# Expert layers of a two-block model: token gather and router with the narrow operand stationary in four column groups

## The reference

```python
def expert_choice_moe(h, w_router, w_gate, w_up, w_down):
    b, s, _ = h.shape
    cap = EC_FACTOR * s // N_EXPERTS
    logits = jnp.einsum('bsd,de->bse', h, w_router, preferred_element_type=jnp.float32)
    aff = jax.nn.softmax(logits, axis=-1)
    gates, idx = lax.top_k(aff.transpose(0, 2, 1), cap)
    b_ix = jnp.arange(b)[:, None, None]
    xs = h[b_ix, idx]
    a = jnp.einsum('becd,edf->becf', xs, w_gate)
    u = jnp.einsum('becd,edf->becf', xs, w_up)
    y = jnp.einsum('becf,efd->becd', jax.nn.silu(a) * u, w_down)
    y = y * gates[..., None].astype(y.dtype)
    return jnp.zeros_like(h).at[b_ix, idx].add(y)
```

## Time and profile before

| | us |
|---|---|
| median of three runs | 2250.71 |
| lowest, highest | 2247.79, 2253.75 |
| span of the profiled execution, first to last instruction | 2245.6 |
| busy in it: PE matmuls, PE weight loads, DVE, ACT | 2025.5, 1382.8, 894.7, 718.1 |
| mean granted TensorE clock (1.00 is 2.4 GHz, 0.50 is 1.2 GHz) | 0.936 |
| moved by DMA, mean rate | 592.33 MB, 264 GB/s |

### The profile page before, as it was taken

The page is one execution under the profiler, slowest core; times in us unless marked ns, Lnnn a source line. Parts: engine busy times, 40 slices in busy tenths (PEclk is TensorE's granted clock), DMA queues, the critical chain, the costliest instruction groups (busy, mean ns, idle before and its releaser), DMA issues.

```text
span 2245.6 us, 38410 instructions
## 1 busy us (share of the span) xinstructions
PE 2025.5 (90%) x17052; PEld 1382.8 (62%) x17052; DVE 894.7 (40%) x1280; ACT 718.1 (32%) x1015; POOL 40.7 (2%) x65
## 2 busy tenths in 40 slices
PE   7999988887879999987777879999999999999998
PEld 6888433333327887433333329575899796758996
DVE  6444211010106444111111117547677475476774
ACT  5444111111115454111111115424444453244442
POOL 1000000000001000000000000000000000000000
PEclk9999898788889999888888889999999999999999
DMA  9246899999997256999999996023754360227540
GB/s 325 74 152 261 370 426 429 429 428 427 429 427 274 75 188 281 385 428 428 428 429 428 428 413 246 16 79 112 236 188 169 103 232 4 89 101 228 187 178 19
DMA packets 139668, 592.33 MB, mean 264 GB/s; under 512 B 5745, under 2 KB 59201, under 8 KB 114449
## 3 DMA queue, kind: packets, MB, share of 16 engines
q1 hardware_dynamic: 138432, 586.67, 65.9%
q0 software_dynamic: 1104, 3.70, 0.5%
HBM read 589.30 MB, written 1.05 MB: 263 GB/s over the span
## 4 chain that ended last, share of the span: by engine, by line
PE 68%; DMA 24%; DVE 3%; ACT 2%; issue 1%; SPq 1%; DVEq 0%; POOLq 0%; ACTq 0%; POOL 0%
PE ps L578 36%; DMA ring<-in_w_up 23%; PE ps L1182 11%; PE ps L2191 3%; PE ps L2006 2%; PE ps L904 2%; PE ps L2240 1%; PE ps L1205 1%; PE ps L1144 1%; DMA ring<-in_w_in 1%; PE ps L1214 1%; PE ps L595 1%; PE ps L1003 1%; PE ps L1099 1%; PE ps L1079 1%
## 5 line engine op out<-in xcount | busy, mean ns | idle before, releaser
L1182 PE MATMUL ps<-ring,area 128*32 128x512 f32 x1920 | 308.0, 714 | 124.5 <-DMA ring<-in_w_up 124.5
L554 DVE TENSOR_TENSOR ring_lo<-ring,slab_hi 128x2048 fp32r<-128x2048 f32 x136 | 311.3, 2291 | 227.0 <-ACT slab_hi L549 226.9
L549 ACT ACTIVATE slab_hi<-ring 128x2048 fp32r<-128x2048 f32 x136 | 260.0, 1913 | 287.2 <-PE ps L578 266.3
L1182 PEld LDWEIGHTS ps<-ring,area 128*32 128x32 f32 x1920 | 72.8, 128 | 314.5 <-DMA ring<-in_w_up 156.7
L578 PE MATMUL ps<-hT_hi,slab_hi 128*128 128x256 f32 x832 | 234.7, 282 | 3.0 <-DVE hT_lo L571 1.5
L578 PE MATMUL ps<-hT_lo,slab_hi 128*128 128x256 f32 x832 | 233.4, 280 | 0.0
L578 PE MATMUL ps<-hT_hi,ring_lo 128*128 128x256 f32 x832 | 232.5, 280 | 0.0
L1771 DVE TENSOR_TENSOR area<-ps,par 128x256 f32<-128x256 f32 x32 | 13.6, 424 | 480.2 <-PE ps L1144 480.2
L1421 ACT ACTIVATE area<-ps 128x512 f32<-128x512 f32 x32 | 19.1, 597 | 536.9 <-PE ps L1182 536.9
L1205 PE MATMUL ps<-ring,area 128*32 128x512 f32 x992 | 158.1, 794 | 31.6 <-DVE area L1791 29.8
L578 PEld LDWEIGHTS ps<-hT_hi,slab_hi 128*128 128x128 f32 x832 | 156.0, 188 | 4.2 <-issue 2.2
(11 more groups left out here) (384 smaller groups left out, 3147.6 us busy)
## 6 DMA issues: line engine op xcount, KB each, us to landing
ring<-in_w_up SPq DMA_DIRECT2D x62, 2048.0 KB, 20.4
ring<-in_w_down SPq DMA_DIRECT2D x62, 2048.0 KB, 21.6
ring<-in_w_gate SPq DMA_DIRECT2D x56, 2048.0 KB, 15.2
ring<-in_w_ffn_up SPq DMA_DIRECT2D x44, 1024.0 KB, 7.8
ring<-in_w_in SPq DMA_DIRECT2D x18, 2048.0 KB, 10.1
ring<-in_w_ffn_down SPq DMA_DIRECT2D x10, 2048.0 KB, 7.8
ring<-in_xattn_w_kv SPq DMA_DIRECT2D x8, 2048.0 KB, 16.7
area<-in_w_gate SPq DMA_DIRECT2D x6, 2048.0 KB, 15.1
```

Source lines behind the costliest of these rows:

```text
L549: return m.nc.scalar.activation(hi, whole, ACT.Copy)
L554: return m.nc.vector.tensor_tensor(lo, whole, hi, ALU.subtract)
L1182: ins = mm(ps[32 * g:32 * g + CAP, 1, :], m.tokT[:, k, :], gate_up[i][:, k % 4, (g % 2) * BANK:(g % 2 + 1) * BANK], start=k == 0, stop=k = ...
```

## The change

Four edits, all in the experts:

1. The router turns its operands round: 32 router columns (those of two neighbouring chunks, of which one half is what is wanted) are stationary, 256 tokens of `hT` move, in four column groups of the array, one chunk each; the second half adds to the same PSUM bank. DVE copies the 128x256 result to SBUF, and two matmuls with a constant `expert_sum` add the four groups and turn them. One of the four copies of the residual (`into_sums`) stands before these two, another behind them; the other two stay behind the turn of the affinities.
2. The gather turns its operands round too: `onehot` (32 columns) stationary, 256 features of `xn` moving, four column groups, 8 matmuls. DVE copies the result to SBUF (`tok_rows`), PE turns it with two transposes (`turn_tokens`), and DVE scales it into `tokT`. In the loop these transposes stand behind those of gate and up.
3. The first maxima and the first replacement of the search read PSUM directly; the copy goes.
4. For expert 0 the turn of `gated` is issued behind the eighth matmul of gate and up instead of ahead of the first.

```diff
+    def into_sums(nh, t):
+        mm(ps[:, 4 + 2 * nh + t, :], m.ident, m.x[:, t, nh * BANK:(nh + 1) * BANK], start=True, stop=False, skip_group_check=True)
...
-        for t in range(NT):
-            for k in range(4 * half, 4 * half + 4):
-                ins = mm(ps[:, 4 + t, 0:E], m.hT[:, k, t * P:(t + 1) * P], router[:, k, :], start=k == 0, stop=k == KD - 1)
+        for g in range(4):
+            k = 4 * half + g
+            ins = mm(ps[CAP * g:CAP * g + CAP, 4, 0:T], router[:, (k - g % 2) * E:(k - g % 2) * E + CAP], m.hT[:, k, :],
+                     start=half == 0, stop=half == 1)
...
+    into_sums(1, 0)
+    pe.wait_ge(*at("router_rows", l))
+    for t in range(NT):
+        ins = mm(ps[:, 5, t * E:(t + 1) * E], m.router_rows[:, t * P:(t + 1) * P], m.const("expert_sum"), start=True, stop=True)
+    ins.then_inc(s("router_full"), 1)
+    into_sums(1, 1)
     pe.wait_ge(*at("aff_rows", l))
...
-        for k in range(KD):
-            for t in range(NT):
-                ins = mm(ps[:, 2, k * CAP:(k + 1) * CAP], m.xn[:, t, k * P:(k + 1) * P], m.onehot[:, t, :],
+        for t in range(NT):
+            for g in range(4):
+                ins = mm(ps[CAP * g:CAP * g + CAP, 2, 0:T], m.onehot[:, t, :], m.xn[:, t, g * T:(g + 1) * T],
                          start=t == 0, stop=t == NT - 1)
...
+    def turn_tokens(n):
+        pe.wait_ge(s("tok_rows"), n)
+        for c in range(2):
+            ins = nc.tensor.transpose(ps[:, 2, T + c * P:T + (c + 1) * P], m.tok_rows[:, c * P:(c + 1) * P], m.ident)
+        ins.then_inc(s("tokens_T"), 1)
...
-        pe.wait_ge(s("gated"), n)
-        for t in range(NT):
-            ins = nc.tensor.transpose(ps[:, 3, t * P:(t + 1) * P], m.gated[:, t, :], m.ident)
-        ins.then_inc(s("pick_T"), 1)
+        if not first:
+            turn_places(n)
...
                 if first and k == 1 and g == 3:
                     ins.then_inc(s("first_rows_used"), 1)
+                    turn_places(n)
...
         ins.then_inc(m.s("gu_T"), 1)
+        if not last:
+            turn_tokens(n + 1)
         pe.wait_ge(m.s("hid_cols"), n)
...
-    v.tensor_copy(work[:, 0, :], ps[0:E, 0, 0:T])
-    dve.drain()
     for r in range(CAP // 8):
-        v.max(best, work[:, r % 2, :])
+        left = work[:, r % 2, :] if r else ps[0:E, 0, 0:T]
+        v.max(best, left)
         dve.drain()
-        v.match_replace(work[:, 1 - r % 2, :], best, work[:, r % 2, :], -1.0)
+        v.match_replace(work[:, 1 - r % 2, :], best, left, -1.0)
...
         dve.wait_ge(s("tok_full"), n)
-        v.tensor_tensor(m.tokT, ps[:, 2, 0:KD * CAP].rearrange("p (k c) -> p k c", c=CAP), bc(m.par1("ffn_g"), CAP), ALU.mult)\
-            .then_inc(s("tok_cols"), 1)
+        v.tensor_copy(m.tok_rows, ps[:, 2, 0:T]).then_inc(s("tok_rows"), 1)
+        dve.wait_ge(s("tokens_T"), n)
+        v.tensor_tensor(m.tokT.rearrange("p (g c) n -> p c g n", c=2), ps[:, 2, T:].rearrange("p (c g n) -> p c g n", c=2, n=CAP),
+                        bc(m.par1("ffn_g").rearrange("p (g c) -> p c g", c=2), CAP), ALU.mult).then_inc(s("tok_cols"), 1)
```

More of the change, by code:

```diff
@@ L144, in constants @@
     put("iota_slot", np.broadcast_to(i % CAP + 1, (P, P)))
+    even = np.arange(E) == i[:, None] % CAP
+    odd = np.arange(E) == i[:, None] % CAP - E
+    put("expert_sum", np.where((i[:, None] // CAP) % 2 == 0, even, odd))
     put("causal", np.where(i[None, :] <= i[:, None], 0.0, -1e30))
@@ L316 @@
 group("mem_dve", first=[("xs_max", 2), ("xp_rows", 2), ("xpT_d", 2), ("xo_cols_d", 4)])
-group("route_pe", first=[("router_full", 2), ("aff_T", 1), ("top_T", 1)])
+group("route_pe", first=[("router_parts", 1), ("router_full", 1), ("aff_T", 1), ("top_T", 1)])
 group("route_act", first=[("router_exp", 2)])
 group("x_perm", first=[("x_perm", 4)])
-group("route_dve", first=[("router_max", 1), ("aff_rows", 1), ("top_found", 1), ("topc_set", 1)])
+group("route_dve", first=[("router_rows", 1), ("router_max", 1), ("aff_rows", 1), ("top_found", 1), ("topc_set", 1)])
 group("acc_full", first=[("acc_full", 2)])
-for n in ("onehot", "gated", "tok_full", "pick_T", "gu_full", "gu_T", "tok_cols", "hid_cols", "pick", "gu_rows", "gate_silu",
+for n in ("onehot", "gated", "tok_full", "tok_rows", "tokens_T", "pick_T", "gu_full", "gu_T", "tok_cols", "hid_cols", "pick", "gu_rows", "gate_silu",
           "dn_rows_a", "dn_rows_d"):
@@ L1111, in tensor_experts @@
     mm = nc.tensor.matmul
-    router = m.par1("router").rearrange("p (k e) -> p k e", e=E)
+    router = m.par1("router")
+    def into_sums(nh, t):
+        mm(ps[:, 4 + 2 * nh + t, :], m.ident, m.x[:, t, nh * BANK:(nh + 1) * BANK], start=True, stop=False, skip_group_check=True)
     for half in range(2):
@@ L1128, in tensor_experts @@
     ins.then_inc(s("aff_T"), 1)
-    for nh in range(2):
-        for t in range(NT):
-            mm(ps[:, 4 + 2 * nh + t, :], m.ident, m.x[:, t, nh * BANK:(nh + 1) * BANK], start=True, stop=False,
-               skip_group_check=True)
+    for t in range(NT):
+        into_sums(0, t)
     pe.wait_ge(*at("top_found", l))
@@ L1141, in gather, with turn_places @@
         pe.wait_ge(s("onehot"), n)
-        for k in range(KD):
-            for t in range(NT):
-                ins = mm(ps[:, 2, k * CAP:(k + 1) * CAP], m.xn[:, t, k * P:(k + 1) * P], m.onehot[:, t, :],
+        for t in range(NT):
+            for g in range(4):
+                ins = mm(ps[CAP * g:CAP * g + CAP, 2, 0:T], m.onehot[:, t, :], m.xn[:, t, g * T:(g + 1) * T],
                          start=t == 0, stop=t == NT - 1)
-                if behind_up and k == 0 and t == 0:
+                if behind_up and g == 0 and t == 0:
                     ins.then_inc(m.free[3], 1)
         ins.then_inc(s("tok_full"), 1)
+    def turn_tokens(n):
[3 more added lines that the diff above has]
+        ins.then_inc(s("tokens_T"), 1)
+    def turn_places(n):
+        pe.wait_ge(s("gated"), n)
+        for t in range(NT):
+            ins = nc.tensor.transpose(ps[:, 3, t * P:(t + 1) * P], m.gated[:, t, :], m.ident)
+        ins.then_inc(s("pick_T"), 1)
     def expert(e, first=False, second=False, third=False, last=False):
@@ L1222, in tensor_experts @@
     gather(l * E + 1, behind_up=False)
+    turn_tokens(l * E + 1)
     expert(0, first=True)
```

18 lines of the change are left out of this document (10 added, 8 removed).

## The result

The changed kernel takes 2238.66 us in the median of four runs (2235.53 to 2242.52), the kernel before, beside it, 2252.23 (2247.79 to 2255.91): a ratio of 0.9949, 95% interval 0.9930 to 0.9967. Three more sets of runs gave 0.9938 (0.9924 to 0.9952), 0.9951 (0.9934 to 0.9968) and 0.9951 (0.9935 to 0.9966). The two profiled executions tell less: spans of 2245.6 and 2237.9 us, 7.7 apart. The profiled execution of the changed kernel took 2239.7 us, so 1.8 us lie around its span. The ratios leave out two executions in a slow state, one of `router_only` (4885 us) and one of `after_warm` (3339 us).

What follows compares the result with a forecast made beforehand. Weight loads bound the expert layers, so only the route to their restart counts. Terms 1.4 + 0.2 + 0.8 + 0.8 + 2.4 - 0.5 = 5.1 us took the median from 2250.7 to 2245.6, range 2240.8 to 2250.

Steps and rivals of the forecast that it cites:

- the one place that counts: Start of each layer's experts, where the DMA stands still: 7.8 us lost in layer 1, 5.6 in layer 2.
- Rival 3: Matmuls in column groups, gather and router: the groups don't run together, 11.6 us slower, 2262.3; chance 0.05.
- The sum: Route to the restart of weight loads, both layers: all terms together save 5.1 us, 2.55 per layer.
- the router's first half: Router, up to its second half: a shorter weight stream lets the transposes start earlier; 0.68 us per layer, 1.4 in all.
- the first rounds: Expert 0's first two gate and up rounds: 3.7 us in both layers after the longer wait, a loss of 0.5.
- the search: Top search after the router: dropping the copy and reading PSUM directly saves 0.4 us per layer, 0.8 in all.
- the term Gather: Expert 0's gather to its first matmul: 1.6 us saved at half clock, 4.1 at full, weighed to 2.4.
- the prediction's terms for the router and its clock: Both router halves: 1.4 and 0.2 us saved, plus 0.8 for an even chance of full clock in layer 1.
- the premium for PSUM: First maxima and replacement of the search: reading PSUM instead of SBUF costs 0.09 us for both.
- Rival 1: Gather and first rounds: PE keeps full clock, gain 8.5 us, 2242.2; chance 0.34.
- Rival 2: End of a layer after its last down slab: low clock costs up to 5.4 us, 2251.0; chance 0.09.
- the 0.17: Switches from column groups to the whole array: leaving the groups costs 0.17 us, one such added switch per layer.

Runs made afterwards that it cites:

- router_only: The kernel before with only the new router and two residual copies moved ahead, gather and search old; 0.9998 (0.9985 to 1.0011) of before.
- after_warm: The changed kernel with six unread matmuls of 256 columns, five during the search and one before the gather; 0.9946 (0.9927 to 0.9965) of before.
- gather_loop: The kernel before with only the fifteen loop gathers of each layer turned, expert 0's gather old; 1.0010 (0.9998 to 1.0022) of before.
- after_slow: The changed kernel with eight more unused maxima ahead of the search; 0.9978 (0.9968 to 0.9988) of before, median 2244.94 us.
- gather_first: The kernel before with only expert 0's gather turned in each layer, the loop's gathers old; 0.9963 (0.9950 to 0.9976) of before.
- old_first: The changed kernel with the old gather for expert 0; 0.9975 (0.9965 to 0.9985) of before, median 2241.58 us.
- after_third: The changed kernel without any edit, run again for a third profile; median 2237.15 us, routes 42.0 us in sum.

## Why the prediction was wrong

**The bound and the one place that counts: right in the main.** The loads run without a break, the loop's gathers alone are worth nothing (`gather_loop`, PE 32 us less busy in 285 at the same 429 GB/s), and a microsecond on the route comes out as about one in the time (`after_slow`). Rival 3 fell with the first row of the new gather, 1.93 us for 16 records in groups.

**The sum against its own profile: near, and partly by luck.** The routes of the first two profiles stand 47.4 - 41.9 = 5.5 us apart, where the sum gave 5.1. The new parts cost what was worked out: 0.71 for the router's first half in layer 1, 3.7 for the half-clock gather, 3.7 for the first rounds. But the terms miss in both directions. From this pair the router gave 2.9 us (2.4 in the sum), the search 1.4 (0.8), the gather 1.6 (2.4, a mean over two clocks of which the lower one came), the way to the gather -0.1 (0) and the first rounds -0.3 (-0.5).

**What failed is the step from this profile to the median, first of all in the term Gather, which was mis-sized.** It priced the old gather by the rows of one execution, "4.62 us, and 4.37", and took that for what before costs, though the same paragraph says that the clock decides between such prices for the new one. In three profiles of before, the way from gather to expert 0 was 4.62, 4.37, 6.63, 6.81, 4.45 and 6.93 us, mean 5.6; of the changed kernel it was 3.68 each time. The term is 2 x (5.63 - 3.68) = 3.9 us, not 2.4. The run that changes nothing else says the same more strongly: `gather_first` gained 8 us (5.4 to 11.2), where Gather and the first rounds together were put at 1.9.

The means of three profiles against four by leg, in both layers together: maxima 2 x (5.82 - 4.43) = 2.8 (the prediction's terms for the router and its clock gave 1.4 + 0.2 + 0.8 = 2.4), search 1.4 (0.8: the copy's 0.49 per layer, without the premium for PSUM, and 0.2 from the turn of the affinities, which comes with the new router, as 2.71 and 2.70 us in `router_only` show), to the gather -0.1, gather 3.9 (2.4), first rounds 0.1 (-0.5). Together 49.7 - 41.6 = **8.1 us**, 3.0 more than the sum; half of that is the gather. The prediction left open what the 5.1 us between span and median are; 1.8 lie around the span, and the other 3.3 were a profiled execution shorter than the median, a hint that its route was a short one.

**Rival 1 had the size of the route's gain and the wrong cause.** It gave 8.5 us, by luck, from a clock that the new route keeps. The new route doesn't keep it (0.66 over 227 to 235); the old one had lost it earlier in three of the four gathers of the other two profiles than in the first profile. Rival 2, a layer's end at the low level, was not seen: the stretch from the last up slab of layer 1 to `x` ready in layer 2 was 223.4 to 223.5 us in before and 223.3 to 224.3 in the changed kernel.

**Whether the parts add, the times don't tell; in the routes they don't.** Gathers of expert 0 alone 8 us, router alone 0, search 0 to 5, and all together 11 to 14: with intervals of 3 us each, that could still be a sum. The routes show more. The router takes 2.8 us off its leg, and in `router_only` the old gather behind it is longer by more than that. That the router's gain comes to light only with the new gather is argued from these legs; no run had just these two.

**What stays open.** The route explains 8.1 of 11 to 14 us. The stretch from the start to `x` ready in layer 1 was 219.9, 218.9 and 219.7 us in before and 217.4, 217.6, 218.1 and 218.8 in the changed kernel, another 1.5 us, though the change does nothing there but add 16 columns of constants. The other kernels without these constants had 218.1 to 219.2, the others with them 217.2 to 218.9; whether that is chance, the few profiles don't tell. For the rest, 1 to 4 us, the sum had no term, and its cause is open. It isn't mere scatter of the medians, since `after_slow` and `old_first` gain 5 to 6 us at the old length of the route. And `gather_first`, whose profile shows the route of the changed kernel (41.9), is 6 us slower than it. One reading is that the three profiles of before caught short executions: their spans, 2244.2 on average, lie 3.3 under the 2247.5 that the medians of before leave without the 1.8 around the span, so its usual route may be longer than 49.7. No further profile tells. Nor did any run put unread matmuls ahead of the old gather, which would show its price at a kept clock.

## What to carry to other kernels

Where a stream of loads is the bound, look for the one stretch in which it stands still, and count only what shortens the way to its restart. A short stretch behind a wait has several prices, by the clock that TensorE happens to have; one profile shows one of them, so price both kernels at both levels and weigh them, the old one too. And test such edits together as well as apart: behind an edit that left PE idle for longer (`router_only`), the next step on it was dearer.

## What the runs showed of the hardware that was not expected

- Keeping PE busy was not enough to keep its clock. The old gather (128x128 weights for 32 columns of data) filled PE without a gap from 236.40, and the granted clock fell to 0.50 after some 3 us of it (windows of `before`, 236.40 to 241). The same 32 records took 3.94 and 6.29 us in two executions of one kernel, and 7.01 where PE had waited for longer before them.
- Six unread matmuls of 256 columns (PE busy 6.8 of 8 us) did nothing for the clock: 0.71 over 229 to 233, as in after_third without them. Nine of up to 512 columns (11.7 of 12 us) held it to expert 0, and there nearly halved what followed: gather 1.07 instead of 1.93 us, first rounds 1.99 instead of 3.70.
- Eight maxima from PSUM took 0.42 us, as from SBUF (224.08 against the earlier trace rows).
- Going from column groups to the whole array cost little: the router's round started at 219.78, and the whole-array matmul behind it at 220.35, 0.57 us later, where two passes of 256 columns (0.21 each by the rows of 512) would let it start after 0.43. So this row leaves 0.14 us for the switch, near the 0.17 that the prediction took for it in its last paragraph before the sum. The Trainium skill (TensorEngine Tiling, section Key Properties) says that changing the tiling mode drains TensorE; this row agrees with it and does not prove it.
